# Two layers and a second block on one core: the last gate units, the post-norm and the next four tiles by token halves

## The reference

```python
def rms_norm(x, gain):
    xf = x.astype(jnp.float32)
    y = xf * lax.rsqrt(jnp.mean(xf * xf, axis=-1, keepdims=True) + RMS_EPS)
    return (y * gain.astype(jnp.float32)).astype(x.dtype)
...
    for i in range(DEPTH):                       # DEPTH = 2
        h = rms_norm(x, norm_mix_pre[i])
        z = h @ w_in[i]
...
        o_b = fourier_mix(h)
...
        x = x + rms_norm(ff, norm_ffn_post[i])
        e = (p[i] @ w_ple_proj[i]) * jax.nn.sigmoid(x @ w_ple_gate[i])
        x = x + rms_norm(e, norm_ple[i])
    return x
```

## Time and profile before

| | us |
|---|---|
| median of 3 runs | 2806.81 |
| lowest, highest | 2804.27, 2807.64 |
| profiled execution, its own time | 2804.86 |
| its span | 2802.8 |
| PE busy | 2696.7 (96% of the span) |
| DVE busy, ACT busy, POOL busy | 1438.3, 1125.4, 411.3 |

### The profile page before, as it was taken

One profiled execution on the slowest core, in us unless ns is written; L12 is line 12 of the kernel. 1 busy time (PEld: TensorE's weight loads), 2 busy tenths in 40 slices (PEclk: granted clock), 3 DMA queues, 4 the chain that ended last, 5 costly groups with the idle time before them and its releaser, 6 DMA issues. The chain is left out here.

```text
span 2802.8 us, 36888 instructions
## 1 busy us (share of the span) xinstructions
PE 2696.7 (96%) x13520; PEld 2181.0 (78%) x13520; DVE 1438.3 (51%) x2072; ACT 1125.4 (40%) x1759; POOL 411.3 (15%) x320
## 2 busy tenths in 40 slices
PE   8999999999999899999999999999998899899997
PEld 6876778888887787677888888776686588788886
DVE  6656644434324665665453432475588636543323
ACT  6345544322224544554332222443524535522221
POOL 5100002211103310000221110331101012311101
PEclk9999999999999999999999999999999999999999
DMA  4320123222232232012322222222231122123232
GB/s 154 129 81 31 46 77 119 74 92 94 100 105 92 83 127 84 31 46 76 120 71 94 92 103 105 92 88 75 78 120 61 61 95 86 46 90 105 90 105 90
DMA packets 37518, 245.92 MB, mean 88 GB/s; under 512 B 4608, under 2 KB 5632, under 8 KB 8448
## 3 DMA queue, kind: packets, MB, share of 16 engines
q1 hardware_dynamic: 33632, 239.09, 24.2%
q10 hardware_dynamic: 3744, 4.93, 0.5%
HBM read 241.91 MB, written 2.10 MB: 87 GB/s over the span
## 5 line engine op out<-in xcount | busy, mean ns | idle before, releaser
L564 PE MATMUL bank<-h_hi,w_hi 128*128 128x512 f32 x1928 | 764.1, 396 | 7.4 <-DVEq L1594 3.9
L566 PE MATMUL bank<-h_hi,w_lo 128*128 128x512 f32 x1928 | 752.9, 390 | 0.0
L565 PE MATMUL bank<-h_lo,w_hi 128*128 128x512 f32 x1928 | 752.3, 390 | 0.0
L1556 DVE TENSOR_TENSOR w_lo<-raw,w_hi 128x2048 fp32r<-128x2048 f32 x133 | 308.3, 2321 | 356.8 <-ACT w_hi L1081 356.1
L564 PEld LDWEIGHTS bank<-h_hi,w_hi 128*128 128x128 f32 x1928 | 362.7, 188 | 94.1 <-issue 11.6
L566 PEld LDWEIGHTS bank<-h_hi,w_lo 128*128 128x128 f32 x1928 | 362.7, 188 | 77.0
L565 PEld LDWEIGHTS bank<-h_lo,w_hi 128*128 128x128 f32 x1928 | 362.9, 188 | 73.5 <-issue 1.4
L1081 ACT ACTIVATE w_hi<-raw 128x2048 fp32r<-128x2048 f32 x151 | 288.1, 1912 | 244.2 <-PE bank L566 235.8
L1568 DVE TENSOR_TENSOR w_lo<-raw,w_hi 128x2048 fp32r<-128x2048 f32 x60 | 137.6, 2292 | 156.5 <-ACT w_hi L1296 156.5
L564 PE MATMUL bank<-a_hi,w_hi 128*128 128x512 f32 x528 | 205.4, 389 | 0.0
L565 PE MATMUL bank<-a_lo,w_hi 128*128 128x512 f32 x528 | 205.4, 389 | 0.0
(11 more groups left out here) (423 smaller groups left out, 4622.2 us busy)
## 6 DMA issues: line engine op xcount, KB each, us to landing
raw<-in_stream SPq DMA_DIRECT2D x226, 1024.0 KB, 4.8
x<-in_xT SPq DMA_DIRECT2D x4, 512.0 KB, 9.0
out_T<-x ACTq DMA_DIRECT2D x8, 256.0 KB, 2.1
p_f<-in_pT ACTq DMA_DIRECT2D x2, 512.0 KB, 4.2
memf<-in_memT ACTq DMA_DIRECT2D x1, 1024.0 KB, 5.6
cst_sb<-in_cst ACTq DMA_DIRECT2D x1, 407.0 KB, 7.4
pos_i<-in_pos ACTq DMA_DIRECT2D x1, 258.0 KB, 6.2
g_in<-in_gains ACTq DMA_DIRECT2D x3, 4.0 KB, 1.8
```

The lines of the kernel that those rows point to most:

```text
L564: nc.tensor.matmul(ps, wh, xh, start=start, stop=False)
L565: nc.tensor.matmul(ps, wh, xl, start=False, stop=False)
L566: return nc.tensor.matmul(ps, wl, xh, start=False, stop=stop)
L1556: nc.vector.tensor_tensor(lo[:, :], raw[v % 2][:, :], hi[:, :].bitcast(F32), ALU.subtract).then_inc(lo_ready, 1)
```

## The change

The last four gate tiles are computed as four half units: unit 4 is tokens 0 to 255 of tiles 4 and 5, unit 5 the same tokens of tiles 6 and 7, units 6 and 7 are tokens 256 to 511 of the same pairs. Gate, squares, sums, root, scaling, addition to x and the rounding follow by token halves. `begin` on PE does its four tiles by halves as well: first tokens 0 to 255 of tiles 0 and 1 (over all k), then of tiles 2 and 3, then the other half. Its first step of a layer takes over the closing sum of squares of the layer before. On ACT and DVE the steps of units 6 and 7 stand between the steps m of the first half. The weight unit that has a buffer of its own is now the first of z1a and z2 instead of the second. `norm_begun` makes the factor by halves and splits the second weight unit at its end instead of at its start. Three counted but empty tiles, which keep the bank numbers in step, move from "ple" to "uq". The layer loop is written out on every engine. At the program's start x is loaded in eight pieces by halves.

```diff
 HALVED = {
     "wout": [2, 4, 7, 8],
+    "ple": [2, 4, 7, 8],
+    "z1a": [0, 4],
...
+    if name == "z2":
+        out[0:2] = [("T", 0), ("T", 4)]
...
         EARLY = {
-            (1, "z1a"): [None, second],
-            (2, "z2"): [None, second],
+            (1, "z1a"): [second, None],
+            (2, "z2"): [second, None],
...
-            def begin(c, st):
+            def begin(c, st, ending=None):
                 u0 = c.base[st]["U"]
...
+                for half in range(2):
+                    at = cols(half)
+                    for p in range(2):
+                        if half == 0:
+                            pe.wait_ge(lo_ready, c.at("U", st, p + 1))
+                        ps = free_bank(c, st, 2 * half + p)
+                        hi, lo = home(c, u0 + p)
+                        for k in range(KD):
+                            if p == 0:
+                                pe.wait_ge(raw_split, c.begun("W", KD * half + k + 1))
+                            for g in range(2):
+                                b = slice((8 * g + k) * P, (8 * g + k + 1) * P)
+                                mm = mac_at(ps[:, cols(g)], hi[:, b], lo[:, b], raw_x_hi[:, k, at], raw_x_lo[:, k, at],
+                                            k == 0 and g == 0, k == KD - 1 and g == 1)
+                            if (half, p, k) == (0, 0, 3) and ending is not None:
+                                half_sum(ending, "ple", 1)
+                            if half == 1 and k == 1:
...
+                                    square_sum(sq_tree, c.begun("Q", p + 1), sq_x[:, j, cols(p)], j == 0, j == 1, ps=HALF_SS[p])
+                        mm.then_inc(tile_done, 1)
...
                 run(c, "ple", lambda n, j: (h_hi[:, j, :], h_lo[:, j, :], (raw_split, c.at("W", "xple", j + 1)) if n == 0 else None),
-                    together=0)
-                project_sum(c, "ple", sq_ready, "SQ")
-                pe.sem_inc(tile_done, NO_TILES)
-
-            with pe.Fori(0, DEPTH) as L:
+                    last=4, together=0)
+                last_units(c, "ple", lambda k, at: h_hi[:, k, at], lambda k, at: h_lo[:, k, at], 6)
+
+            for L in range(DEPTH):
...
             def norm_begun(c, st, blocks):
 
-                for u in range(2):
-                    split_unit(c, st, u)
...
+                begun_root(c, 0)
+                split_unit(c, st, 0)
+                begun_root(c, 1)
                 begun_hi(c, range(blocks))
+                split_unit(c, st, 1)
...
+                ple_gate(4)
+                split_unit(c, "ple", 2)
+                ple_squares(4)
+                ple_gate(5)
                 log_table()
-                root("ple", c, 2, S, D)
+                ple_squares(5)
+                half_root(c, "ple", 0, 3, HALF_RSTD[0][:, 0:HALF])
+                act.preload_act_table(ACT.Sigmoid)
+                ple_gate(6)
                 act.wait_ge(gain_loaded, L * 16 + 32)
                 for m in range(KD):
-                    begin_hi(m, (x_ready, c.at("X", "post3", m + 1)))
+                    begin_hi(m, 0, (x_ready, c.at("X", "post3", m + 1)))
+                    if m == 1:
+                        ple_squares(6)
+                    elif m == 2:
+                        ple_gate(7)
+                    elif m == 3:
+                        ple_squares(7)
+                    elif m == 4:
+                        split_unit(c, "ple", 3)
+                log_table()
+                half_root(c, "ple", 1, 6, HALF_RSTD[1][:, 0:HALF])
+                for m in range(KD // 2):
+                    begin_squares(m, 0)
+                for m in range(KD):
+                    begin_hi(m, 1, (x_ready, c.at("X", "post3", KD + m + 1)))
+                    if m % 2 == 1:
+                        begin_squares(m // 2, 1)
...
+                for half in range(2):
+                    at = cols(half)
+                    dve.wait_ge(rms_ready, c.at("N", "post3", half + 1))
+                    for m in range(KD + 2):
...
+                        if half == 0 and m == 1:
+                            gate_ple(6)
+                        elif half == 0 and m == 3:
+                            gate_ple(7)
+                        elif half == 0 and m == 6:
+                            split_unit(c, "ple", 3)
+                        elif half == 1 and m == 2:
+                            add_begun(0, c.at("SQ", "begin", 4))
+                        if m >= 2:
+                            begin_lo(m - 2, half, c.at("W", "begin", KD * half + m - 1))
+                add_begun(1, c.at("SQ", "begin", 8))
```

More of the change, by code:

```diff
@@ L1047, in unit_steps @@
                 for n, end in enumerate(ends):
-                    if st in SPLIT_AHEAD and n == len(ends) - 1 and end == u:
-                        split(u)
                     if end == u:
                         evac(n)
-                if u < max(ends) or st not in SPLIT_LATER and st not in SPLIT_AHEAD:
+                if u < max(ends) or st not in SPLIT_LATER:
                     split(u)
@@ L1869, in first_low @@
                 nc.vector.tensor_tensor(lo[:, :], raw[v][:, :], hi[:, :].bitcast(F32), ALU.subtract).then_inc(lo_ready, 1)
-            first_low(0, w_hi[0], w_lo[0])
-            for m in range(KD):
-                begin_lo(m, m + 1)
-            first_low(1, *second)
-            add_begun(KD)
+            first_low(0, *second)
+            for half in range(2):
+                for m in range(KD):
+                    begin_lo(m, half, KD * half + m + 1)
+                    if half == 1 and m == 2:
+                        add_begun(0, 4)
+                if half == 0:
+                    first_low(1, w_hi[1], w_lo[1])
+            add_begun(1, 8)
             start_steps = chain["n"]
@@ L1999, in first_block @@
-                post(c, "ple", "post3", 1, "ple", e, lo=lambda m: begin_lo(m, c.at("W", "begin", m + 1)))
-                add_begun(c.at("SQ", "begin", KD))
+                    if n < 4:
+                        part, by = e[:, n, :], sg[:, n % 2, :]
+                    else:
+                        half, two = (n - 4) // 2, n % 2
+                        part = e[:, 4 + 2 * two:6 + 2 * two, cols(half)]
+                        by = res[:, n - 4, :].rearrange("p (i s) -> p i s", i=2)
+                    nc.vector.tensor_tensor(part, part, by, ALU.mult).then_inc(tile_free, 1)
@@ L2001, in first_block @@
+                add_begun(1, c.at("SQ", "begin", 8))
                 assert chain["n"] <= CHAIN_PER_LAYER
                 dve.sem_inc(vchain, CHAIN_PER_LAYER - chain["n"])
-            with dve.Fori(0, DEPTH) as L:
+            for L in range(DEPTH):
                 first_block(L)
@@ L2277, in _ @@
             turns()
-            with pool.Fori(0, DEPTH) as L:
+            for L in range(DEPTH):
                 c = Counts(BASE1, L)
```

187 lines of the change are left out of this document (105 added, 82 removed).

## The result

| | before | after |
|---|---|---|
| median of 5 runs, us | 2807.64 | 2822.78 |
| lowest, highest | 2804.27, 2808.77 | 2821.49, 2824.56 |
| profiled execution, its span | 2802.8 | 2822.8 |

The change makes the kernel slower: the ratio is 1.0057 (95% interval 1.0045 to 1.0069). The forecast was 2822. Run once more beside other kernels, the same kernel stood at 1.0071 (1.0057 to 1.0085), so 16 to 20 us.

A forecast was written before the change was run, and what follows sets the result against it. Bound: PE's work (busy 96% of the span) plus its stands and half clock. Terms 6.4 + 4.9 + 1.7 + 4.8 - 0.5 = +17.3 us on 2804.86 gave 2822; own range 2817 to 2827 (0.60), wider range 2810 to 2829.

The forecast's parts named there:

- PE's arrival at `begin`: End of layer: PE finishes half unit 7 at 25.2 us, where `begin` started at 30.7; 0.8 us stand included.
- T: End of half unit 7 on PE, at 25.2 us counted from the end of the fourth gate tile.
- The chain to k = 4: After unit 7, serial steps on ACT, DVE and POOL take 10.8 us until k = 4; PE stands 6.6 us in pieces.
- The start of "four1": After an end of layer, "four1" can start at 58.3 us, against 57.0 before.
- "four1": First-block layer starts: the late weight unit on DVE delays the fifth tile; third group +6.4 us in layer 1, +4.9 in layer 0.
- The second block: Its start: 1.3 us from the end of layer and 0.4 for the first h, +1.7 us.
- The clock: Half clock behind four new stands: 1.7 us each at two ends, 0.7 each in two "four1", 4.8 us in all.
- The loop: Layer loop written out removes register instructions ahead of waits: 0 to -2 us, taken as -0.5.
- layer 0's start: No end of layer comes before; third group of "four1" at about 51.4 instead of 46.37, +4.9 us.
- the first end with the start behind it: End of layer 0 and start of layer 1: third group of "four1" at 72.3 against 65.9, +6.4 us without clock.
- three of the rivals: Not named; those using 11.7 or 2.8: halves as in "wout" 2792 (0.08), only "four1" stands 2804 (0.05), longer slow clock 2829 (0.10).

The follow-up runs named there:

- the experiment on the ends: Changed kernel with unit 7's sigmoid, multiplication, squares and next weight unit behind the first half's roundings, and PE's second closing sum later; 2805.5 us, 1.0003.
- the second execution: The changed kernel run again, unaltered; 2824.9 us, 1.0071 to the kernel before.
- the run with spare matmuls: Changed kernel with 26 spare half-width matmuls ahead of k = 4 and 32 ahead of the fifth four1 tile; 2817.9 us, 1.0042.
- the late weight unit: Changed kernel with the second weight unit of first-block layer starts split later, behind four1's eighth (ACT) and twelfth (DVE) small tile; 2819.5 us, 1.0046.
- only the weight unit behind the first half: Changed kernel with only the weight unit behind unit 7 moved behind the first half's roundings on ACT and DVE; 2821.3 us, 1.0058.
- the kernel before with spare matmuls: Kernel before with the layer loop written out and 5 and 18 spare matmuls in the stand at each end of layer; 2803.7 us, 0.9993.
- the kernel with the loop alone: Kernel before with nothing but the layer loop written out on PE, DVE, ACT and POOL; 2802.1 us, 0.9989.
- the reordered kernel: Changed kernel with ends reordered, late weight unit moved, POOL's squares additions later and first two tiles scaled ahead of the second half's factor; 2794.3 us, 0.9965.

## Why the prediction was right

Step by step, in the prediction's own terms; stretches are from the table.

- *PE's arrival at `begin`.* Said: T = 25.2 for 30.7, 5.5 us earlier. Measured: 66.39 to 60.89, 5.50, with the 0.61 us stand ahead of half unit 5 (said 0.8).
- *The chain to k = 4.* Said: T + 10.8, with stands of 1.3, about 1 and 4.2. Measured: 932.51 - 921.77 = 10.74, with 1.15, 0.48 and 3.79. These are 5.4 us of standing where I had 6.6, since PE's own steps and the sum take 5.3 there and not 4.2; the chain runs on the other engines, so its length does not change by that. Every link has the place that the order gave it, and the experiment on the ends shows that the order is the cause: the same work in another order has no stand for a rounding at the ends.
- *The start of "four1"* after `begin`. Said 58.3 - 25.2 = 33.1; measured 34.08, of which 0.4 is half clock.
- *"four1".* Said: fifth tile 9.7 us (the parts that it is added up from give 9.5) and third group 14.0 after the first tile. Measured: 8.88 and 14.42 (970.27 - 955.85); PE stood 4.70. In layer 0 the third group was said to come at 51.4; its row:

```profile
51.77 0.29 PE L568 MATMUL bank<-w_hi,h_hi 128*128 128x288 f32 x1
```

  That it came so near is partly luck: the first tile started at 37.11 where I had 37.8, and the third group 14.7 us after it where I had 13.6, with more half clock than in the second execution (37.86 and 13.5 there).

- *The second block.* Said +1.7 and 1.7 for the clock; measured +5.0 (5.56 gained, 10.55 lost), 1.7 of it the clock by the run with spare matmuls. The start of the stage was mis-sized by 1.6 us. Some 1.0 of these are the wait for the first h: behind `begin`, the way to the score is 1.4 us longer (44.11 to 45.48), with 0.99 us of PE waiting for `h_lo`, where I had 0.4.
- *The clock.* Said: 4.8 us for the four stands; measured 4.8 against the first profile and 4.0 against the second, and divided otherwise: the ends 0.4 and 1.7, "four1" 1.2 and 1.5 (0.4 in the second profile), where I had 1.7 each and 0.7 each. That the sum fell on 4.8 is luck.
- *The loop.* Said: 0 to -2, taken -0.5. Measured -3.0 (-0.6 to -5.6). This term was too small. The two profiles differ by 2.5 us, of which 2.1 lie between `begin` and ob of the two layers, where the reasoning by neighbours in `project_norm` did not look; 0.7 of these are the shorter half clock. That the rest is the register instructions between engines that hand each other short pieces is not shown.
- *Not foreseen:* 2.9 us between the indexer's first score and the last sum, where the change touches nothing but addresses. 2.3 of them (17.19 to 19.49 us between the same instructions of the two) follow one wait, of 0.69 us in both kernels. Behind it before, and after:

```profile
2227.51 1.09 PE L758 MATMUL bank<-pT,vw 128*64 128x128 f32 x16 [0.69 <-ACT pT L1237]
...
2229.35 0.40 PE L564 MATMUL bank<-h_hi,w_hi 128*128 128x512 f32 x1
2230.04 0.39 PE L564 MATMUL bank<-h_hi,w_hi 128*128 128x512 f32 x1
```

```profile
2244.70 1.98 PE L768 MATMUL bank<-pT,vw 128*64 128x128 f32 x16 [0.69 <-ACT pT L1259]
...
2248.05 0.63 PE L571 MATMUL bank<-h_hi,w_hi 128*128 128x512 f32 x1
2249.33 0.60 PE L571 MATMUL bank<-h_hi,w_hi 128*128 128x512 f32 x1
```

Three matmuls start in 0.69 us there and in 1.28 here. Of the eleven profiles on record, six have the half clock behind this wait: those of the changed kernel, of its variants with the late weight unit, with only the weight unit behind the first half and with spare matmuls, and that of the kernel before with spare matmuls, whose ends are unchanged otherwise. Five have not, the three with the ends in another order among them. So it does not belong to the halving, and part of what a reordering seems to gain lies here. What decides which of the many short waits of the attention is followed by half clock stays open.

The sum was +17.3 on the profiled execution. The two profiled executions differ by 19.7 (2804.86 and 2824.56), the medians by 15.1 and, in the later comparison, 20.7. Held against the kernel with the loop alone, layer 0's start costs 5.9 us, the first end with the start behind it 9.3 and the second 5.2; the terms with their share of the clock said 5.6, 8.8 and 3.4. So they were right to about 2 us each, and that the median fell on 2822.8 is partly luck: the loop's surplus goes against the half clock that I did not foresee and the second block's start.

One statement of the prediction fell, on which the upper bound of the clock term and three of the rivals rested, though not the sum. I wrote that an end of layer costs 11.7 us, 8.9 of standing and 2.8 of slow clock, and that halving can attack them. Of the 2.8 at most 0.7 are the clock's: with the clock held up the rest is lost to the pace of DVE's scaling and rounding. Halving does get at them, by another way, since half tiles are rounded ahead of PE. In the reordered kernel the first end and the start behind it, from "pp" to ob, take 121.07 us, against 124.29 with the loop alone, and the second block's 132.92 against 136.65. That is 3 to 4 us of the 11.7. By the reckoning of the prediction the rest goes into half-width matmuls and the closing sums that once stood in the gap; no run takes them apart.

## What to carry to other kernels

When work is halved so that the first half's tail can run beside the second half's start, look first at each in-order engine: any step that needs the end of the second half and stands ahead of a step of the first half brings the old stand back. Here such steps (the sigmoid with its multiplication, the squares, a weight unit) cost 14.5 us at two ends, and with the order worked out the kernel became faster than before the change. A step that prepares something for a later stage belongs behind the work for which the next stage already waits. And before a slow clock behind a stand is counted as a loss, ask what PE would wait for at full clock.

## What the runs showed of the hardware

Half clock behind a stand has no fixed price, and no fixed length: the granted clock stayed at 0.50 for 3.1 to 6.2 us, and at each place it cost more where it stayed longer. Behind the old stand of 5.4 us, where the roundings came at 1.69 us a step, it cost nothing at the end where it lasted 3.4 us and 0.6 us where it lasted 5.5. Behind two stands of 3.79 us with the same work behind them it lasted 3.1 and 6.2 us and cost 0.4 and 1.7. Behind two of 4.7 us it lasted 5.1 and 5.6 and cost 1.2 and 1.5; in a second execution of the same kernel it lasted 3.1 us behind the latter and cost 0.4. What sets the length is not shown.

It also moved: behind the same wait of 0.69 us the matmuls ran at full clock in the kernel before and at half in the changed one, in both of its profiles. A change at one place, even one that only adds spare matmuls there, can thus go with 2 to 4 us at another that it does not touch, which is as much as the smaller edits here are worth.
